# The first norm of a two-block transformer kernel: the second tile's scaling moves from GpSimd to VectorE, and the zero products around the first transposes are redistributed

## What is computed

```python
def rmsnorm(x, g):
    xf = x.astype(jnp.float32)
    y = xf * lax.rsqrt(jnp.mean(xf * xf, axis=-1, keepdims=True) + RMS_EPS)
    return (y * g.astype(jnp.float32)).astype(x.dtype)

def mixer(h, w_in, b_f, conv_w, w_branch, w_out):
    proj = jnp.einsum("bsd,dn->bsn", h, w_in)
    q, k, v, f_logit, g_b, g_c, hc, gate_conv, gate_attn = jnp.split(proj, _SPLITS, axis=-1)
    ...

h = rmsnorm(x, norm_mix_pre[l])
m = mixer(h, w_in[l], b_f[l], conv_w[l], w_branch[l], w_out[l])
```

## Time and profile before

| | |
|---|---|
| Median of three runs | 972.84 us (972.52 to 973.36) |
| Profiled execution | 973.3 us |
| Its span in the trace | 972.0 us, so 1.3 us lie around it |
| TensorE matmul busy | 961.8 us (99%) |
| VectorE busy | 726.4 us (75%) |
| ScalarE busy | 530.7 us (55%) |
| GpSimd busy | 35.5 us (4%) |
| Memory traffic | 225.68 MB, mean 232 GB/s |

### The profile page before, as it was taken

The page is one execution under the profiler, slowest core; times in us unless marked ns, Lnnn a source line. Parts: engine busy times, 40 slices in busy tenths (PEclk is TensorE's granted clock), DMA queues, the critical chain, the costliest instruction groups (busy, mean ns, idle before and its releaser), DMA issues.

```text
span 972.0 us, 14072 instructions
## 1 busy us (share of the span) xinstructions
PE 961.8 (99%) x5768; PEld 847.5 (87%) x5768; DVE 726.4 (75%) x1102; ACT 530.7 (55%) x808; POOL 35.5 (4%) x59
## 2 busy tenths in 40 slices
PE   9999999999999999999999999999999999999997
PEld 7999999888888887998888888887998788888886
DVE  7799867788778766978678878766786678666563
ACT  6645543564554555655565454555766675445451
POOL 2000000020000001000000000001000100000000
PEclk9999999999999999999999999999999999999999
DMA  9777688469977753767467677764643256658511
GB/s 363 301 292 260 260 303 307 174 201 213 398 290 298 288 201 131 253 261 266 187 248 298 247 295 263 278 241 132 237 136 125 87 220 241 232 182 317 174 44 44
DMA packets 33153, 225.68 MB, mean 232 GB/s; under 512 B 4058, under 2 KB 4341, under 8 KB 6720
## 3 DMA queue, kind: packets, MB, share of 16 engines
q1 hardware_dynamic: 30960, 219.43, 61.7%
q0 software_dynamic: 1696, 5.08, 1.9%
q10 hardware_dynamic: 432, 0.26, 0.1%
HBM read 223.49 MB, written 1.26 MB: 231 GB/s over the span
## 4 chain that ended last, share of the span: by engine, by line
PE 96%; DVE 2%; ACT 1%; POOL 0%; issue 0%; DVEq 0%
PE psum L620 22%; PE psum L622 12%; PE psum L659 10%; PE psum L660 10%; PE psum L661 10%; PE psum L582 8%; PE psum L583 7%; PE psum L584 7%; PE psum L883 2%; PE psum L731 1%; PE psum L730 1%; PE psum L732 1%; PE psum L317 1%; PE psum L951 1%; PE psum L1149 1%; ACT work L331 1%
## 5 line engine op out<-in xcount | busy, mean ns | idle before, releaser
L509 DVE TENSOR_TENSOR low<-raw,high 128x2048 fp32r<-128x2048 f32 (+1 forms) x160 | 361.1, 2275 | 108.4 <-ACT high L503 108.4
L503 ACT ACTIVATE high<-raw 128x2048 fp32r<-128x2048 f32 (+1 forms) x160 | 299.2, 1897 | 18.2 <-DMA raw<-in_gate_up 6.8
L620 PE MATMUL psum<-h_both,high 128*128 128x512 f32 x936 | 234.0, 392 | 0.0
L620 PEld LDWEIGHTS psum<-h_both,high 128*128 128x128 f32 x936 | 169.8, 189 | 32.0 <-issue 0.5
L582 PE MATMUL psum<-h_both,high 128*128 128x256 f32 x544 | 156.6, 288 | 0.5 <-DVE low L509 0.5
L583 PE MATMUL psum<-h_both,high 128*128 128x256 f32 x544 | 153.9, 283 | 0.0
L584 PE MATMUL psum<-h_both,low 128*128 128x256 f32 x544 | 153.8, 283 | 0.0
L622 PEld LDWEIGHTS psum<-h_both,low 128*128 128x128 f32 x960 | 130.8, 190 | 9.1
L622 PE MATMUL psum<-h_both,low 128*128 128x256 f32 x960 | 133.9, 282 | 0.0
L659 PE MATMUL psum<-high,y_hi 128*128 128x512 f32 x328 | 129.1, 394 | 0.5 <-DVE y_lo L973 0.5
L660 PE MATMUL psum<-low,y_hi 128*128 128x512 f32 x328 | 128.0, 390 | 0.0
(11 more groups left out here) (177 smaller groups left out, 1018.4 us busy)
## 6 DMA issues: line engine op xcount, KB each, us to landing
raw<-in_gate_up SPq DMA_DIRECT2D x66, 1024.0 KB, 5.7
raw<-in_ada SPq DMA_DIRECT2D x48, 1024.0 KB, 4.9
raw<-in_down SPq DMA_DIRECT2D x33, 1024.0 KB, 5.4
raw<-in_mix SPq DMA_DIRECT2D x14, 1024.0 KB, 6.9
raw<-in_moba_qk SPq DMA_DIRECT2D x8, 1024.0 KB, 5.2
raw<-in_diff_qk SPq DMA_DIRECT2D x8, 1024.0 KB, 5.0
raw<-in_qk SPq DMA_DIRECT2D x4, 1024.0 KB, 15.8
raw<-in_branch SPq DMA_DIRECT2D x4, 1024.0 KB, 5.9
```

Source lines behind the costliest of these rows:

```text
L503: nc.scalar.activation(high[n % N_HI][:, s], raw[i % N_RAW][:, s], ACT.Copy).then_inc(*rounded.up(n if key is None else key))
L509: nc.vector.tensor_tensor(low[i % N_RAW][:, s], raw[i % N_RAW][:, s], high[n % N_HI][:, s].bitcast(F32), ALU.subtract).then_inc(*rest.up(key))
L620: nc.tensor.matmul(o[:, :], a, h_both[:, k, :, :], start=k == 0, stop=False)
```

## The change

Three edits, all in the first 15 us of the program. GpSimd's two multiplications for tile 1 are taken out, with their semaphore. VectorE calls `dve_scale_x("in", 1)` behind the split of tile 0's first four column blocks and ahead of the remainder of the first weight slab. TensorE's products of zeros become 13 ahead of the first transposes (17 before) and 14 behind them (11 before).

```diff
@@ def build_program @@
-        scaled_pool = sig("scaled_pool")
         powed, small_pool = sig("powed"), sig("small_pool")
@@ def pe_turn @@
                 for k in range(a, b):
                     yield from pe.wait_ge(ident_in, "ident")
-                    yield from pe.wait_ge(*((scaled_pool, k // 4) if stage == "in" and t else (scaled, (stage, t, k // 4))))
+                    yield from pe.wait_ge(scaled, (stage, t, k // 4))
@@ def tensor @@
             yield from pe.wait_ge(small_dve, "blank")
-            keep_busy(17)
+            keep_busy(13)
             yield from pe_turn("in", 0)
-            keep_busy(11)
+            keep_busy(14)
@@ def vector @@
             yield from dve_join(("x", "in", 1), 1, 0)
             for a, b in PIECES[0][0]:
                 yield from dve_split_h("in", 0, a, b)
+            yield from dve_scale_x("in", 1)
             for i, kind, m in dve.items(0):
                 yield from dve_rest(0, 0, slice(0, SLAB // 2), (0, "a"))
@@ def gpsimd @@
             for t in range(NT):
                 yield from pool_power(joined, ("x", "in", t), stat[:, 2 * t:2 * t + 1], 1)
-            yield from pool.wait_ge(powed, ("x", "in", 1))
-            for c in range(2):
-                nc.gpsimd.tensor_scalar(work_a[:, half_of(1, c)], x_res[:, 1, c * 512:(c + 1) * 512], stat[:, 2:3], None,
-                                        ALU.mult).then_inc(*scaled_pool.up(c))
             nc.gpsimd.dma_start(c_row[:, :], dram["c"].partition_broadcast(P)).then_inc(*c_in.up("c", by=16))
```

## The result

The changed kernel takes 975.08 us, the median of 12 runs (973.85 to 976.08), the kernel before 973.12 us beside it (12 runs, 971.79 to 973.49): a ratio of 1.0021 (after to before; over 1 is slower), 95% interval 1.0014 to 1.0029. Forecast were 972.2 us and the range 971.5 to 973.5.

A forecast was written before the change was run, and what follows sets the result against it. TensorE, busy 961.8 of 972.0 us, was taken to bound the kernel, through its first real matmul. From the median 972.84, minus 0.45 (fewer zeros) and 0.17 (GpSimd's leaving less VectorE's scaling), came 972.2 us; range 971.5 to 973.5.

The forecast's parts named there:

- What bounds the kernel: TensorE's matmuls hold 96% of the chain; the forecast hangs on when the first real matmul starts.
- Part 1: TensorE's zeros ahead of the first transposes: four fewer gain 0.68 us against the profile, 0.45 taken against the median.
- Part 2: VectorE's four split instructions: without GpSimd's multiplications beside them 1.34 us instead of 2.31, a gain of 0.97.
- Part 3: VectorE's scaling of tile 1 ahead of the first slab's remainder: adds 0.80 us to the path.
- Rival (a): VectorE's casts stay slow, the first beside GpSimd's power: 0.43 to 0.97 us back, 972.6 to 973.2; chance 0.20.
- Sum: First real matmul on TensorE at 11.62 us instead of 12.47, 0.85 earlier.
- What comes later: Later slabs: GpSimd's DMAs, issued 3.1 us earlier, cost nothing if slab 3's rounding slips less than about a microsecond.
- Rival (c): Earlier GpSimd transfers push slab 3 beyond its slack: up to 2 us lost, 973 to 974.3; chance 0.04.
- Rival (b): TensorE's clock does not rise in front: 973.9 halfway, at worst about 975 us; chance 0.08.

The follow-up runs named there:

- the zeros alone: Kernel before with 13 products of zeros in front and 14 behind the first transposes, GpSimd still scaling tile 1: 972.63 us, ratio 0.9999.
- the zeros back: Changed kernel with products of zeros as before, 17 and 11, GpSimd's transfers still early: 974.03 us, ratio 1.0019.
- one DMA early: Changed kernel with GpSimd's first DMA (c_row) still early and the other three held until about 11.6 us: 973.28 us, ratio 1.0005.
- the logits first: Changed kernel with VectorE's copy of the logits moved ahead of the remainder of slab 3, transfers still early: 974.21 us, ratio 1.0016.
- the DMAs held: Changed kernel with GpSimd's four DMAs waiting for the first half of slab 0's remainder, about 11.6 us: 972.43 us, ratio 0.9997.

## Why the prediction was wrong, point by point

**What bounds the kernel** was right: every microsecond of this case is one in which TensorE stands still or runs slowly.

**Part 1, four products less.** Right for the profiled execution: the 26 records end where the transposes can begin. Wrong as a gain of 0.45 on the median: the zeros alone changed the median by nothing (972.63 against 972.57). The profile of before was an execution at the upper end of its runs, 973.3 against medians of 972.55 to 973.12 in the sessions here. The forecast's own condition was the deciding one: where the clock rises early the 17 products cost nothing, and the trace with the zeros back shows such an execution. The runs of the kernel before fall into two groups themselves, in one session 13 between 972.35 and 972.82 us and 8 between 973.01 and 973.29, some 0.7 apart, and with 13 products in front the upper group is not seen (highest 972.87 of 11). So the 0.68 is real in some executions, and it depends on the session whether the median is one of them. With an early transpose VectorE also starts its cast ahead of GpSimd, and most of the contention of part 2 is then not there to be removed.

**Part 2, GpSimd leaves.** The term of 0.97 was exact in the trace (1.33 us for four instructions), and that GpSimd was the cause is shown by all traces without its multiplications, where, with the scaling behind them, the same four take 1.33 or 1.34 us; where VectorE was first GpSimd itself took 4.86 us. But beside the new zeros only 0.30 of the 0.97 was to be had (1.63 in the run with the zeros alone), against the 0.87 of part 3, so with part 1 in place the other two lengthen the way to the first real matmul by 0.56 us (3.46 against 2.90 from the first cast); the run with the zeros alone pays for it with a stop of 0.4 at tile 1's transposes. The rule of the Trainium skill ("SBUF — State Buffer", section "SBUF: two separate sides") that whoever starts first gets the shared ports agrees with both traces in direction; that the loser waits for the whole instruction does not agree with the cast of 0.67 us, which ended at 9.57 beside a GpSimd instruction that had begun at 8.74 and took about 1.6. Rival (a), a slow cast beside GpSimd's power, did not occur: 0.29 us at 8.26, the power running from 8.07 to 8.63.

**Part 3, VectorE scales.** Right, 0.87 us on the path (9.59 to 10.46, forecast 0.80). The two instructions take 0.94 or 0.95 us in the five traces in which GpSimd issues its second and third DMA beside them, and 0.88 in the others.

**Sum.** The first real matmul was forecast at 11.62 and measured at 11.72.

**What comes later** is the step that failed, in the sentence that the earlier DMAs cost nothing as long as slab 3 is delayed by less than about a microsecond. The slack itself was nearly right: ScalarE waited 2.44, 2.62 and 2.13 us for slab 3 in three traces (changed kernel twice, zeros back), and TensorE then 1.0, 1.2 and 0.7 at L1170, so about 1.4 us are free; with one DMA early it waited 1.14, and TensorE did not wait at L1170. But the delay was put below that without an estimate from the traffic. It was 3.5 us in landing between the first traces of the two kernels (2.4 to 3.9 over the traces of all runs), for DMAs that were moved by 3.3. Rival (c) named the mechanism and its worst price, up to 2 us, and was given a chance of 0.04. It should have been the forecast: the weights' queue alone took 99.0% of the DMA engines from 12 to 16 us, GpSimd's queue would be active for some 12 us, and slab 3 lands inside exactly that stretch. Also, the slack of slab 4 was counted to its use by TensorE, "over ten us away", and not to what ScalarE has queued behind its rounding; the run with the logits first shows 1.6 us on that path.

**What no rival had**: the stop does not cost its own length alone. In more than half of the executions another 1.5 us are lost; the traced execution of that group lost it by a fall of the clock behind the stop, and the mean granted clock of the others agrees. Rival (b) looked for the clock at the start, where the runs show no loss. The sum in place of mine: the spans with the DMAs held and of the changed kernel's first trace are 971.1 and 972.6 us; of the 1.5 between them 1.0 + 0.3 are the two stops and 0.13 the first real matmul (11.59 and 11.72). That is the lower group. The 1.5 between the groups comes on top, and the median fell into the upper group. That it did, and not into the lower as with the zeros back, can be chance: 7 of 12 and 5 of 11 are not clearly different.

## What to carry to other kernels

Taking work off a queue moves everything behind it, and a DMA issue is work too: when the traffic is full, a transfer that nobody needs yet should wait for an event of the kernel, not for whatever stood ahead of it by chance. Count the slack of a late slab to the first instruction queued behind its consumer on each engine, not to its own use. A stop of about a microsecond ahead of tiny products can cost more than its length, because the clock may fall behind it; and one profiled execution that lies above the median shows costs that the typical execution does not have.

## What the hardware showed that was not expected

GpSimd's queue took about a third of the DMA engines' time against the weights' queue while it was active, and in single stretches more. In 12 to 24 us its share was 35.1% in the changed kernel (24.3% to 54.2% in its stretches of 2 us):

```profile
q1 hardware_dynamic: 542, 3.15, 63.8%
q0 software_dynamic: 475, 1.65, 35.1%
```

and 22.5% before, where it began at about 16 us (33.1% from 16 to 24):

```profile
q1 hardware_dynamic: 626, 3.82, 78.2%
q0 software_dynamic: 298, 1.04, 22.5%
```

TensorE's clock fell to 1.2 GHz behind a stop of 1.2 us and eight products of 8 columns (second trace of the changed kernel). It did not fall behind a stop of 1.0 us and the same products (first trace), nor behind the stop of 1.37 us between products of zeros and full-size matmuls. Why it falls in one execution and not in another is not settled by these traces.
